# First stage of a hybrid decoder step on one core: order of the first loads, of the turning of x, and of the sum of squares

## The chip, the cores and the metric

The kernel runs on one core of one Trainium2 chip. The metric is the device time in microseconds of one execution; the time before is the median of 3 runs.

## What is computed

One layer of a decoder trunk runs over 256 prompt tokens and 8 sequences of 4 sampled tokens, 288 columns in all (T = 288). The reference, cut to the part that the first stage of the kernel computes (D_MODEL = 2048, all in float32):

```python
mod = (jax.nn.silu(c) @ p['w_ada'] + p['b_ada']).reshape(bsz, 6, 1, D_MODEL)
shift1, scale1, gate1, shift2, scale2, gate2 = (mod[:, i] for i in range(6))

def _rmsnorm(x, g):
    y = x32 * lax.rsqrt(jnp.mean(x32 * x32, axis=-1, keepdims=True) + RMS_EPS)
    return (y * g.astype(jnp.float32)).astype(x.dtype)

h = _rmsnorm(x, p['norm1_g']) * (1 + scale1) + shift1
z = h @ p['w_in']
```

`w_ada` is 2048 x 12288, `w_in` is 2048 x 10528. The rest of the layer (the two token mixers, the gated merge, the output projection, the second norm with the ConvFFN, the final norm) is the same in both kernels and starts after the first stage.

## The kernel before

Everything is written by hand for five instruction streams (`sp`, `pool`, `act`, `dve`, `pe`), with semaphores between them. The order of the work is the order in which the lines are written.

Weights come in slabs. A slab of `w_ada` is 256 rows by 512 columns (0.5 MB), two k tiles. `ada_load(s)` (L594 ff.) sends for slab s, `ada_slab(s)` on TensorE multiplies it with `scT`, the turned silu(c), into a bank of PSUM. Eight slabs (ADA_K) make 512 columns of mod. `ada_place(s)` gives a slab its place: for the first 16 these are four quarters of `kpage` and four of `ada_d`, used in turn, from slab 16 on `ada_x` (which lies over `xnat`, the natural x) and `ada_d`. `ada_load(s)` for s >= 8 waits until slab s - 8 has been used (`ada_used`); slab 16 waits until all twelve banks of x have been read.

After eight slabs ScalarE copies the bank to `adr` (`ada_rows`), TensorE turns it (`ada_turn`) and VectorE adds the bias into `mod` (`ada_cols`).

x arrives with tokens on the partitions and has to be turned. `turn_bank(bi)` turns four 128-column pieces of x into one PSUM bank (four banks in rotation), and `read_bank(bi)` on VectorE copies the bank to `xT`. There are twelve such banks, three token tiles (the last has 32 tokens) by four quarters of the columns, in the order of the list `banks`; a thirteenth, `par`, holds the small parameters, which the list of loads `PARAM_ROWS` brings to `prow` in 17 small transfers.

ScalarE squares xT by quarters (`squares`), TensorE sums all 16 pieces over the partitions with the matrix "mean" (`means`), ScalarE takes the root (`rms`), VectorE the reciprocal (`rstd`) and x / root (`over_root`, L1406), then `ada_first(0)`, `za_lo(0)`, `ada_first(1)`, `norm_quarter(0)` and `norm_lo(0, 0)`. Here the first product with `w_in` can start.

Of `w_in` the first 3360 columns (stage "za") are computed in 36 units (`za_unit`), each of 36 matmuls of 288 columns, with two slabs of `w_in` of 0.375 MB. Between the units TensorE does two more slabs of `w_ada` (`ada_after`). TensorE does slabs 0 to 19 of `w_ada` ahead of the first unit (AHEAD = 20). The sequence of SyncE's queue sets when each slab is sent for:

```python
            for s in range(4):
                ada_load(s)
            ...
            for s in range(4, 8):
                ada_load(s)
            sp.wait_ge(zeroed, 2)
            for name, (t, r, n) in PARAM_ROWS.items():
            ...
            for s in range(8, ADA_EARLY):
                ada_load(s)
```

Of the kernel before, what the change touches and what calls it, by code (L numbers as in the profile page):

```python
# [24 lines left out]
ALU = mybir.AluOpType  # L25
# [6 lines left out]
P = 128  # L32
# [3 lines left out]
T = TP + NB * TS  # L36
# [96 lines left out]
def build(nc, d):  # L133
    ctx = ExitStack()
    with ctx:  # L135
# [384 lines left out]
        for name, ks, groups in (("za", 2, UNITS), ("rest", RS, KA - 1), ("merge", 8, 4), ("out", 8, 4),  # L520
# [10 lines left out]
        ADA_ROWS1 = 1  # L531


        banks = [("x", (m, q)) for m in range(3) for q in range(4)] + [("par", None), ("sh", None)] \
            + [("cv", q) for q in range(2)]
        BANKS_X = 12
        CV_PARTS = [(0, 5), (5, CV_T)]
        ADA_ORDER = [0, 4, 1, 5, 2, 6, 3, 7]
        M_ROWS = [P, P, NB * TS]
# [41 lines left out]
        def _(sp):  # L581
# [15 lines left out]
            def ada_load(s):  # L597

                place, landed_, _ = ada_place(s)
                col = ADA_ORDER[s // ADA_K] * CH  # L600
                if s >= 8 and not ADA_EARLY <= s < ADA_EARLY + 4:
                    sp.wait_ge(ada_used, s - 7)
                sp.dma_start(place.rearrange("p (t n) -> p t n", t=2),
                             wsrc(d["w_ada"], s % ADA_K * 2 * P, col, CH)).then_inc(landed_, 16)
# [4 lines left out]
                wait = (ada_used, 9 + n) if n < 4 else (slab_lo, n - 3)  # L609
                slab(n, 0, 0, wsrc(d["w_in"], (4 * q + 2 * k) * P, u * QT * P, QT * P), wait)  # L610

            for s in range(4):
                ada_load(s)
            for mt in range(2):
                sp.dma_start(xnat[:, mt, :], d["x_prompt"][0, mt * P:(mt + 1) * P, :]).then_inc(x_in, 16)
            sp.dma_start(xnat[0:NB * TS, 2, :], d["x_sample"].rearrange("b t f -> (b t) f")).then_inc(x_in, 16)
            sp.dma_start(cst[:, P:], d["consts"][:, P:]).then_inc(params_in, 16)
            for s in range(4, 8):
                ada_load(s)
            sp.wait_ge(zeroed, 2)  # L620
            for name, (t, r, n) in PARAM_ROWS.items():
                dst = prow[r:r + n, t, :]
                if name == "mu_shift":
                    sp.dma_start(prow[r:r + n - 1, t, :], d[name][0:(n - 1) * P].rearrange("(r c) -> r c", c=P)).then_inc(params_in, 16)
                    w = ZA - (n - 1) * P
                    sp.dma_start(prow[r + n - 1:r + n, t, 0:w], d[name][(n - 1) * P:ZA].rearrange("(r c) -> r c", r=1)).then_inc(params_in, 16)
                elif name == "rwkv_rk":
                    sp.dma_start(dst, d[name].rearrange("(r a) c -> r (a c)", a=2)).then_inc(params_in, 16)
                elif name.startswith("conv_w"):
                    sp.dma_start(dst, d["conv_w"][int(name[-1]), :].rearrange("(r c) -> r c", c=P)).then_inc(params_in, 16)  # L630
                else:
                    sp.dma_start(dst, d[name].rearrange("(r c) -> r c", c=P)).then_inc(params_in, 16)
            for s in range(8, ADA_EARLY):
                ada_load(s)
            sh0 = (SH_T - 1) * P
            sp.dma_start(shnat[0:NB, 0:sh0], d["state_shift"][:, 0:sh0]).then_inc(states_in, 16)
            sp.dma_start(shnat[NB:2 * NB, 0:ZA - sh0], d["state_shift"][:, sh0:ZA]).then_inc(states_in, 16)
            sp.dma_start(cvnat[:, :], d["state_conv"].rearrange("b r (x k) -> (b r x) k", x=4)).then_inc(x_in, 16)
# [219 lines left out]
        def pbank(b):  # L858
            return ps[:, b, :]
# [85 lines left out]
        def _(act):  # L945
# [2 lines left out]
                return act.activation(o, i, ACT.Copy, **k)  # L948


            act.wait_ge(bank_turned, 1)
            act.activation(scT[:, :, 0:NC], pbank(0)[:, 0:KD * NC].rearrange("p (k c) -> p k c", c=NC), ACT.Silu).then_inc(silu_done, 1)

# [34 lines left out]
            def ada_rows(n):  # L988

                act.wait_ge(ada_used, n * ADA_K + ADA_K)  # L990
                if n:
                    act.wait_ge(ada_turned, n)
                copy(adr[:, :], pbank(6 if n else 5)).then_inc(ada_copied, 1)
# [5 lines left out]
            def za_hi(n):  # L999
                hi("za", G(0, None, n // 2), n % 2, QT * P)  # L1000

            ada_rows(0)
            for q in range(4):
                act.wait_ge(bank_read, BANKS_X - 3 + q)
                squares(0, q)
            act.wait_ge(means_done, 1)
            act.activation(rms[:, :], pbank(0)[:, 0:T], ACT.Sqrt, bias=c("eps_rms")).then_inc(rms_done, 1)
            ada_rows(1)
# [341 lines left out]
        def _(dve):  # L1350
# [131 lines left out]
                    ins = TTn(zs, zs, samp(ps[:, b3 + k, TP:T]), ALU.add)  # L1482
                ins.then_inc(za_in_sbuf, 1)

            for bi in range(BANKS_X + 1):
                read_bank(bi)
            inverse_roots(0)
            for q in range(4):
                own.inc(over_root(0, q))
# [454 lines left out]
        def _(pe):  # L1944
# [69 lines left out]
                if q == 3:  # L2014
                    i.then_inc(means_done, 1)

            for k in range(ADA_K):
                ada_slab(k)
                if k >= 4:
                    for bi in range(2 * k - 8, 2 * k - 6):  # L2020
                        turn_bank(bi)
            for k in range(ADA_K):
                ada_slab(ADA_K + k)
                if k < 2:
                    turn_bank(8 + 2 * k)
                    turn_bank(9 + 2 * k)
                if k == 3:
                    turn_bank(BANKS_X)
                if k >= 4:
                    means(0, k - 4)  # L2030
            ada_turn(1, 7)
            for s in range(ADA_EARLY, AHEAD):
                ada_slab(s)
                if s == ADA_EARLY:
                    pe.wait_ge(ada_in_mod, 1)
                    ada_turn(2, 7)
            pe.wait_ge(rms_done, 1)
            pe.wait_ge(bank_read, BANKS_X + 1)

# [599 lines left out]
```

## Time and profile before

| | |
|---|---|
| median of 3 runs | 2440.32 us (2436.37 to 2441.68) |
| the profiled execution, its own time | 2434.05 us |
| its span, first to last instruction | 2432.2 us |
| mean granted clock of TensorE | 0.973 |
| TensorE matmul busy | 2309.8 us, 95% of the span |
| weight loads busy | 2037.3 us, 84% |
| VectorE busy | 1150.6 us, 47% |
| ScalarE busy | 955.8 us, 39% |

Busy times are shares of the whole span. The queue row "q1" carries what SyncE issues (450.39 MB, 59.1% of the sixteen DMA engines' time), "q10" what ScalarE issues (8.38 MB, 1.0%). The granted clock is given as a share of 2.4 GHz: 1.00 is 2.4, 0.50 is 1.2.

### The profile page before, as it was taken

What the parts mean: (1) busy time and instruction counts of PE and PEld (TensorE: products, weight loads), DVE (VectorE), ACT (ScalarE), POOL (GpSimd) and SP (SyncE); (2) the same over time, 40 slices, a digit from 0 to 9 for tenths busy, and PEclk for the clock granted to TensorE, in tenths of its full rate; (3) what the DMA queues carried; (4) which work ended last, traced back from release to release, by engine and by line L of the source; (5) the groups of instructions that cost most, each with busy time, mean ns of one, the idle gap of its engine ahead of it and who ended that gap; (6) DMA issues with size and microseconds to landing.
All of it is one profiled execution on the core that took longest, in us unless ns stands there. A gap on an engine that the chain in (4) does not pass through costs nothing. (4 is left out here: it accounts for less than half of the span.)

```text
span 2432.2 us, 49500 instructions
## 1 busy us (share of the span) xinstructions
PE 2309.8 (95%) x19762; PEld 2037.3 (84%) x19762; DVE 1150.6 (47%) x1908; ACT 955.8 (39%) x1413; POOL 107.6 (4%) x224
## 2 busy tenths in 40 slices
PE   6999899999999999978998999799999999999998
PEld 3789787878878887645666999799999999999998
DVE  3456635344353543434444555645455555544433
ACT  1433333334343343325433333355454554433333
POOL 0000011010000000100000000000000010000000
PEclk8999999999999999959998999899999999999999
DMA  9885556655666656666997555355555555555544
GB/s 316 276 304 150 150 182 183 187 170 180 185 190 187 183 172 189 209 206 228 342 327 249 157 156 165 100 165 165 165 166 166 166 164 164 164 166 164 164 145 119
DMA packets 326693, 461.17 MB, mean 190 GB/s; under 512 B 37338, under 2 KB 220396, under 8 KB 326076
## 3 DMA queue, kind: packets, MB, share of 16 engines
q1 hardware_dynamic: 318893, 450.39, 59.1%
q10 hardware_dynamic: 7634, 8.38, 1.0%
q8 instruction: 128, 2.10, 0.4%
q14 instruction: 38, 0.30, 0.0%
HBM read 442.83 MB, written 15.86 MB: 189 GB/s over the span
## 5 line engine op out<-in xcount | busy, mean ns | idle before, releaser
L948 ACT ACTIVATE whi<-raw 128x1024 fp32r<-128x1024 f32 (+1 forms) x512 | 526.3, 1028 | 912.3 <-PE ps L1948 882.5
L1948 PE MATMUL ps<-hhi,whi 128*128 128x288 f32 x2736 | 832.6, 304 | 12.1 <-DVE hlo L1447 6.4
L1948 PE MATMUL ps<-hhi,wlo 128*128 128x288 f32 x2736 | 808.4, 295 | 0.0
L1948 PE MATMUL ps<-hlo,whi 128*128 128x288 f32 x2736 | 807.6, 295 | 0.0
L1396 DVE TENSOR_TENSOR wlo<-raw,whi 128x1024 fp32r<-128x1024 f32 (+1 forms) x400 | 470.4, 1177 | 624.6 <-ACT whi L948 624.6
L1948 PEld LDWEIGHTS ps<-hhi,whi 128*128 128x128 f32 x2736 | 515.3, 188 | 76.2 <-issue 55.8
L1948 PEld LDWEIGHTS ps<-hlo,whi 128*128 128x128 f32 x2736 | 515.8, 189 | 1.2
L1948 PEld LDWEIGHTS ps<-hhi,wlo 128*128 128x128 f32 x2736 | 515.2, 188 | 0.0
L1948 PE MATMUL ps<-fhi,whi 128*128 128x288 f32 x704 | 208.0, 295 | 2.8 <-DVE wlo L1396 2.8
L1948 PE MATMUL ps<-fhi,wlo 128*128 128x288 f32 x704 | 207.7, 295 | 0.0
L1948 PE MATMUL ps<-flo,whi 128*128 128x288 f32 x704 | 207.3, 294 | 0.0
L1577 DVE TENSOR_TENSOR wlo<-raw,whi 128x1024 fp32r<-128x1024 f32 x112 | 136.7, 1221 | 109.7 <-ACT whi L948 109.6
L1948 PEld LDWEIGHTS ps<-fhi,whi 128*128 128x128 f32 x704 | 132.1, 188 | 3.6 <-DVE wlo L1396 3.5
L1948 PEld LDWEIGHTS ps<-flo,whi 128*128 128x128 f32 x704 | 132.1, 188 | 0.2
L1948 PEld LDWEIGHTS ps<-fhi,wlo 128*128 128x128 f32 x704 | 132.1, 188 | 0.0
L1948 PE MATMUL ps<-raw,scT 128*32 128x512 f32 x512 | 80.7, 634 | 11.9 <-DMA raw<-in_w_ada 11.9
L1948 PE MATMUL ps<-mhi,whi 128*128 128x288 f32 x256 | 76.4, 298 | 1.6 <-DVE wlo L1396 1.6
L948 ACT ACTIVATE kT<-ps 128x1024 f32<-128x1024 f32 x64 | 64.6, 1019 | 32.6 <-PE ps L2494 32.3
L1948 PE MATMUL ps<-mlo,whi 128*128 128x288 f32 x256 | 75.7, 296 | 0.0
L1948 PE MATMUL ps<-mhi,wlo 128*128 128x288 f32 x256 | 75.2, 294 | 0.0
L948 ACT ACTIVATE Xs<-ps 128x256 f32<-128x256 f32 (+1 forms) x48 | 18.4, 383 | 144.2 <-PE ps L1948 144.0
L1661 DVE TENSOR_TENSOR Tn<-Tn,ps 128x128 f32<-128x128 f32 x40 | 11.5, 288 | 122.5 <-PE ps L1948 122.5
(389 smaller groups left out, 2801.0 us busy)
## 6 DMA issues: line engine op xcount, KB each, us to landing
raw<-in_w_up SPq DMA_DIRECT2D x352, 256.0 KB, 2.9
raw<-in_w_ada SPq DMA_DIRECT2D x128, 512.0 KB, 4.9
raw<-in_w_in SPq DMA_DIRECT2D x112, 512.0 KB, 4.6
raw<-in_w_down SPq DMA_DIRECT2D x88, 512.0 KB, 3.9
kpage<-in_cache_v SPq DMA_DIRECT2D x64, 512.0 KB, 5.1
raw<-in_w_in SPq DMA_DIRECT2D x72, 384.0 KB, 5.4
kpage<-in_cache_k SPq DMA_DIRECT2D x40, 512.0 KB, 5.1
ada_d<-in_w_ada SPq DMA_DIRECT2D x32, 512.0 KB, 4.9
```

What stands on the lines that cost most here:

```text
L948: return act.activation(o, i, ACT.Copy, **k)
L1396: TTn(wlo[:, n % 2, :, 0:width], raw[:, n % 4, :, 0:width], whi[:, n % 2, :, 0:width].bitcast(F32), ALU.subtract).then_inc(slab_lo, 1)
L1577: TTn(wlo[:, n % 2, :, :], raw[:, r, :, :], whi[:, n % 2, :, :].bitcast(F32), ALU.subtract).then_inc(slab_lo, 1)
L1661: TTn(even, even, pbank(1)[:, 0:2 * H].rearrange("p (n t) -> p n t", t=1 << lev), ALU.subtract).then_inc(t_done, 1)
L1948: return pe.matmul(out, lhsT, rhs, start=start, stop=stop, **k)
```

## The change

Five things are changed, all ahead of the first unit of "za".

1. SyncE sends for x (three transfers) ahead of slabs 0 to 3.
2. The 17 small parameter transfers are issued by ScalarE, ahead of its first activation, and no longer by SyncE between slabs 7 and 8. The wait on `zeroed` that stood before them stands now, on SyncE, before the states.
3. The banks of x are in the order of quarters (q outside, token tile inside), and TensorE turns all twelve ahead of slab 0; before, two banks stood behind each of slabs 4 to 9.
4. ScalarE squares a quarter as soon as its three banks are read, ahead of `ada_rows(0)`. VectorE adds the four quarters of squares into the first (three additions of 128 x 1152). TensorE then needs 4 matmuls for the mean, behind slab 5, where it had 16 behind slabs 12 to 15.
5. `ada_turn(1)` stands behind slab 11 and `ada_turn(2)` ahead of slab 16; they stood behind slab 15 and behind slab 16.

```diff
-        banks = [("x", (m, q)) for m in range(3) for q in range(4)] + [("par", None), ("sh", None)] \
+        banks = [("x", (m, q)) for q in range(4) for m in range(3)] + [("par", None), ("sh", None)] \
...
+        SQUARES_SUMMED = 2 + 3
...
-            for s in range(4):
-                ada_load(s)
             for mt in range(2):
                 sp.dma_start(xnat[:, mt, :], d["x_prompt"][0, mt * P:(mt + 1) * P, :]).then_inc(x_in, 16)
             sp.dma_start(xnat[0:NB * TS, 2, :], d["x_sample"].rearrange("b t f -> (b t) f")).then_inc(x_in, 16)
+            for s in range(4):
+                ada_load(s)
             sp.dma_start(cst[:, P:], d["consts"][:, P:]).then_inc(params_in, 16)
             for s in range(4, 8):
                 ada_load(s)
-            sp.wait_ge(zeroed, 2)
-            for name, (t, r, n) in PARAM_ROWS.items():
...
             for s in range(8, ADA_EARLY):
                 ada_load(s)
             sh0 = (SH_T - 1) * P
+            sp.wait_ge(zeroed, 2)
...
+            act.wait_ge(zeroed, 1)
+            for name, (t, r, n) in PARAM_ROWS.items():
...
+            for q in range(4):
+                act.wait_ge(bank_read, 3 * q + 3)
+                squares(0, q)
             ada_rows(0)
-            for q in range(4):
-                act.wait_ge(bank_read, BANKS_X - 3 + q)
-                squares(0, q)
...
-            for bi in range(BANKS_X + 1):
+            for bi in range(BANKS_X):
                 read_bank(bi)
+            for q in range(1, 4):
+                dve.wait_ge(squares_done, q + 1)
+                own(TTn(sqs[0][:, 0:4, :], sqs[0][:, 0:4, :], sqs[0][:, 4 * q:4 * q + 4, :], ALU.add))
+            read_bank(BANKS_X)
...
-            for k in range(ADA_K):
-                ada_slab(k)
-                if k >= 4:
-                    for bi in range(2 * k - 8, 2 * k - 6):
-                        turn_bank(bi)
-            for k in range(ADA_K):
-                ada_slab(ADA_K + k)
-                if k < 2:
-                    turn_bank(8 + 2 * k)
-                    turn_bank(9 + 2 * k)
+            for bi in range(BANKS_X):
+                turn_bank(bi)
+            for k in range(ADA_EARLY):
+                ada_slab(k)
                 if k == 3:
                     turn_bank(BANKS_X)
-                if k >= 4:
-                    means(0, k - 4)
-            ada_turn(1, 7)
+                if k == 5:
+                    pe.wait_ge(dve_done, SQUARES_SUMMED)
+                    for t in range(4):
+                        i = mm(pbank(0)[:, 0:T], c("mean"), sqs[0][:, t, :], t == 0, t == 3)
+                    i.then_inc(means_done, 1)
+                if k == ADA_K + 3:
+                    ada_turn(1, 7)
+            pe.wait_ge(ada_in_mod, 1)
+            ada_turn(2, 7)
             for s in range(ADA_EARLY, AHEAD):
                 ada_slab(s)
-                if s == ADA_EARLY:
-                    pe.wait_ge(ada_in_mod, 1)
-                    ada_turn(2, 7)
```

TensorE, from behind the turning of c to the parameters' bank. `kpage` and `ada_d` in the output's place hold slabs of `w_ada` (two matmuls each), `xnat` is x being turned (four transposes to a bank), `prow` the parameters. Before:

```order
2 L1948 MATMUL ps<-kpage,scT 32x512 x8
3 L1948 MATMUL ps<-ada_d,scT 32x512 x2
4 L1978 MATMUL ps<-cst,xnat 128x128 x8
5 L1948 MATMUL ps<-ada_d,scT 32x512 x2
6 L1978 MATMUL ps<-cst,xnat 128x128 x8
7 L1948 MATMUL ps<-ada_d,scT 32x512 x2
8 L1978 MATMUL ps<-cst,xnat 128x128 x8
9 L1948 MATMUL ps<-ada_d,scT 32x512 x2
10 L1978 MATMUL ps<-cst,xnat 128x128 x8
```

The same place with the change, up to the matmuls of the mean (`sq`):

```order
7 L1985 MATMUL ps<-cst,xnat 128x32 x4
8 L1985 MATMUL ps<-cst,xnat 128x128 x8
9 L1985 MATMUL ps<-cst,xnat 128x32 x4
10 L1955 MATMUL ps<-kpage,scT 32x512 x8
11 L1973 MATMUL ps<-cst,prow 128x128 x4
12 L1955 MATMUL ps<-ada_d,scT 32x512 x4
13 L1955 MATMUL ps<-sq_74,cst 128x288 x4
14 L1955 MATMUL ps<-ada_d,scT 32x512 x4
15 L1955 MATMUL ps<-kpage,scT 32x512 x8
```

All 48 transposes of x stand now ahead of the first slab, and the mean stands between slabs 5 and 6 with 4 matmuls.

SyncE's queue from the constants to the first slabs of `w_in` (`raw`), with the change (before, `kpage` x4 stood ahead of `xnat`, and 17 transfers to `prow` between `ada_d` x4 and the second `kpage` x4):

```order
5 L614 DMA xnat<-in_x_prompt 128x2048 x2
6 L615 DMA xnat<-in_x_sample 32x2048
7 L604 DMA kpage<-in_w_ada 128x2x512 x4
8 L618 DMA cst<-in_consts 128x2643
9 L604 DMA ada_d<-in_w_ada 128x2x512 x4
10 L604 DMA kpage<-in_w_ada 128x2x512 x4
11 L604 DMA ada_d<-in_w_ada 128x2x512 x4
12 L625 DMA shnat<-in_state_shift 8x1664
13 L626 DMA shnat<-in_state_shift 8x1696
14 L627 DMA cvnat<-in_state_conv 64x1408
15 L593 DMA raw<-in_w_in 128x2x384 x4
16 L604 DMA ada_x<-in_w_ada 128x2x512 x4
```

What is loaded ahead of the first unit, and from slab 8 on its order, is as before.

ScalarE, from behind the parameters to the root, with the change (`scT` is silu(c), which every slab and, through a wait, every turning of x stands behind):

```order
12 L946 DMA prow<-in_mu_shift 1x32
13 L952 DMA prow<-in_conv_b 44x128
14 L950 DMA prow<-in_conv_w 44x128 x3
15 L955 ACT_TABLE_LOAD
16 L955 ACTIVATE scT<-ps 128x16x9
17 L968 ACTIVATE sq_74<-xT 128x1152 x4
18 L937 ACTIVATE adr<-ps 128x512
19 L1010 ACT_TABLE_LOAD
20 L1010 ACTIVATE rms<-ps,cst 128x288
```

Silu and its table load stood first on this engine; the 17 issues of small transfers are now ahead of them, and the squares ahead of the first copy to `adr`.

## Rows read from the trace of the kernel before

**Rows 1.** Timeline of TensorE, first stage: start us, duration us, what, count, idle before.

```profile
21.66 1.92 PE L1948 MATMUL ps<-ada_d,scT 128*32 128x512 f32 x4 [9.83 <-DMA ada_d<-in_w_ada]
23.51 1.95 PE L1978 MATMUL ps<-cst,xnat 128*128 128x128 f32 x8
26.37 1.09 PE L1978 MATMUL ps<-cst,xnat 128*128 128x128 f32 x8
...
37.16 2.21 PE L1948 MATMUL ps<-sq,cst 128*128 128x288 f32 x8
...
50.36 1.05 PE L1948 MATMUL ps<-ada_x,scT 128*32 128x512 f32 x4 [0.84 <-ACT adr L948]
56.73 1.88 PE L1948 MATMUL ps<-cst,adr 128*128 128x9 f32 x8 [5.32 <-DVE mod L1388]
58.54 3.63 PE L1948 MATMUL ps<-ada_x,scT 128*32 128x512 f32 x12
64.31 0.37 PE L1948 MATMUL ps<-hhi,whi 128*128 128x288 f32 x1 [2.14 <-DVE hlo L1452]
```

**Rows 2.** Timeline of VectorE, first stage.

```profile
27.07 1.29 DVE L1373 COPY xT<-ps 128x512 f32<-128x512 f32 x2 [0.88 <-PE ps L1978]
...
49.30 1.95 DVE L1401 RECIPROCAL rstd<-rms 128x288 f32<-128x288 f32 x1 [12.32 <-ACT rms L1007]
51.29 5.17 DVE L1406 TENSOR_TENSOR sq<-xT,rstd 128x1152 f32<-128x1152 f32 x4
56.48 0.20 DVE L1388 TENSOR_TENSOR mod<-ps,par 128x36 f32<-128x36 f32 x1
56.60 0.95 DVE L1396 TENSOR_TENSOR wlo<-raw,whi 128x768 fp32r<-128x768 f32 x1
58.65 0.20 DVE L1388 TENSOR_TENSOR mod<-ps,par 128x36 f32<-128x36 f32 x1 [1.10 <-PE ps L1948]
```

**Rows 3.** Timeline of ScalarE, first stage.

```profile
37.53 1.28 ACT L1007 ACT_TABLE_LOAD   x1
48.77 0.50 ACT L1007 ACTIVATE rms<-ps,cst 128x288 f32<-128x288 f32 x1 [9.96 <-PE ps L1948]
```

**Rows 4.** Timeline of SyncE's queue: start and duration of issues.

```profile
10.24 6.84 SPq L632 DMA_DIRECT2D prow<-in_b_ada  x1
```

**Rows 5.** Single transfers: issue ns, start us; us to landing (second: least, median, most of x's three).

```profile
L616 SPq DMA_DIRECT2D xnat<-in_x_sample x1: 432/432/432, 5.1 to 5.1; - x1
...
DMA to landing us min/median/max: 8.5/11.1/12.2
...
L603 SPq DMA_DIRECT2D ada_d<-in_w_ada x1: 2694/2694/2694, 7.5 to 7.5; - x1
...
DMA to landing us min/median/max: 18.4/18.4/18.4
...
L603 SPq DMA_DIRECT2D kpage<-in_w_ada x1: 389/389/389, 23.1 to 23.1; - x1
...
DMA to landing us min/median/max: 6.4/6.4/6.4
...
L592 SPq DMA_DIRECT2D raw<-in_w_in x1: 398/398/398, 32.5 to 32.5; - x1
...
DMA to landing us min/median/max: 12.2/12.2/12.2
```

**Rows 6.** The last slab of w_ada ahead of the first unit, the same columns.

```profile
L603 SPq DMA_DIRECT2D ada_x<-in_w_ada x1: 1792/1792/1792, 41.3 to 41.3; - x1
...
DMA to landing us min/median/max: 12.0/12.0/12.0
```

**Rows 7.** Windows: stretch; busy of PE, PEld, DVE, ACT, POOL; PEclk, DMA share, GB/s.

```profile
14.00:16.00 2.00, 0.00 (x0) 0.00 (x0) 0.00 (x0) 0.00 (x0) 0.00 (x0) 0.77 1.14 219
...
54.00:56.00 2.00, 0.00 (x0) 0.00 (x0) 2.00 (x2) 0.00 (x0) 0.00 (x0) 0.50 1.05 386
...
80.00:90.00 10.00, 10.00 (x79) 8.14 (x78) 3.08 (x5) 4.37 (x9) 0.00 (x0) 1.00 0.88 302
```

More of the change, by code:

```diff
@@ L619, in _ @@
                 ada_load(s)
-            sp.wait_ge(zeroed, 2)
-            for name, (t, r, n) in PARAM_ROWS.items():
[L622 to L632, printed above, removed]
             for s in range(8, ADA_EARLY):
@@ L948, in copy @@
                 return act.activation(o, i, ACT.Copy, **k)
+            act.wait_ge(zeroed, 1)
+            for name, (t, r, n) in PARAM_ROWS.items():
+                dst = prow[r:r + n, t, :]
+                if name == "mu_shift":
+                    act.dma_start(prow[r:r + n - 1, t, :], d[name][0:(n - 1) * P].rearrange("(r c) -> r c", c=P)).then_inc(params_in, 16)
+                    w = ZA - (n - 1) * P
+                    act.dma_start(prow[r + n - 1:r + n, t, 0:w], d[name][(n - 1) * P:ZA].rearrange("(r c) -> r c", r=1)).then_inc(params_in, 16)
+                elif name == "rwkv_rk":
+                    act.dma_start(dst, d[name].rearrange("(r a) c -> r (a c)", a=2)).then_inc(params_in, 16)
+                elif name.startswith("conv_w"):
+                    act.dma_start(dst, d["conv_w"][int(name[-1]), :].rearrange("(r c) -> r c", c=P)).then_inc(params_in, 16)
+                else:
+                    act.dma_start(dst, d[name].rearrange("(r c) -> r c", c=P)).then_inc(params_in, 16)
             act.wait_ge(bank_turned, 1)
```

## Prediction, on record before the changed kernel was run

> **What bounds the kernel now.** The page's section 1 comes first: TensorE is busy for 95% of the span, so time can be won only where it stands still. One such place is the first stage, and the timeline of TensorE shows it [rows 1]: the engine waits until 21.66 us for slab 4 of w_ada, and after slab 16 (50.36, 1.05 us) it does nothing until 56.73, waits again from 62.2 (58.54 + 3.63) and starts the first unit of "za" at 64.31. From there the windows show it busy without a gap, 10.00 of 10 us at full clock, with the DMA engines at 0.88 [rows 7]. So the first stage is worth what the start at 64.31 moves, and nothing else in the program hangs on absolute time.
>
> Next I ask what ends last before 64.31. The timelines of VectorE and ScalarE [rows 2, 3] show one chain: the last mean ends at 48.7, root at 48.77 (0.50), reciprocal 49.30 (1.95), x over root 51.29 (5.17), the first bias 56.48; TensorE turns the second group (56.73, 1.88), bias 58.65, and the normed quarter with its splitting into high and low parts takes until 64.31, 5.66 us after 58.65. 15.6 us of chain, all behind the mean. It is VectorE and ScalarE that bound the start now.
>
> Behind them stands the stream of loads. Landing times are issue plus time to landing [rows 5]: x complete at 5.1 + 12.2 = 17.3, slab 7 at 7.5 + 18.4 = 25.9, slab 8 at 23.1 + 6.4 = 29.5, the first slab of w_in at 32.5 + 12.2 = 44.7, and slab 19, the last that TensorE needs ahead of the first unit, at 41.3 + 12.0 = 53.3 [rows 6]. From 44.7 to 53.3 three slabs of w_in and four of w_ada land, 3.3 MB, that is 1.36 us for a slab of w_ada. The window 54 to 56 has the DMA engines at 1.05 and 386 GB/s while TensorE is idle [rows 7]: the stream has run full all the time. This is the floor under whatever the chain may win.
>
> **The change, part by part.**
>
> *x ahead of slabs 0 to 3.* x lands four slabs sooner: 17.3 - 4 x 1.36 = 11.9, and 12.5 with half a microsecond for the parameters' bytes beside it.
>
> *Parameters on ScalarE.* 17 issues. On SyncE the list took from 10.24 to 23.1; 6.84 of it was the first, which stood before a full queue [rows 4, 5], so the other 16 took 6.0, 0.37 each. On ScalarE 17 x 0.37 = 6.3 us from about 1.4, to 7.7; then the table load (1.28) and silu (0.3, my estimate from the 0.50 of the root, a smaller tile): 9.4. TensorE starts nothing before silu, but x lands at 12.5, so 3 us are left. The issues are hidden by x's landing; without that cover each microsecond of list beyond 10.8 is a microsecond of turning.
> In the stream the list cost more than its 0.19 MB: slab 8 landed 3.6 us behind slab 7, where 1.36 is usual, 2.2 too many. Issued early they fall partly into the first microseconds, before anything large is queued. The ends: the whole 2.2 goes, or nothing. I take 1.0. In a sentence by itself: the Trainium skill, "DMA: Bandwidth & Descriptors", section "Issuing engines are not separate DMA queues", says that transfers from several engines share the same 16 DMA engines and spreading saves only the issuing time; by that the stream would win nothing, slab 19 stays at 53.3 and the gain is one microsecond smaller than below.
>
> *Turning x first.* Twelve banks. When TensorE is warm VectorE sets the pace, 1.29 for two banks [rows 2], 0.65 each; cold, the transposes do, 1.95 for two, against 1.09 warm [rows 1]. Between 6 and 12.5 the engine is idle, and an idle engine lost its clock before (0.77 in 14 to 16, 0.50 in 54 to 56) [rows 7]. Ends 7.8 (all warm) and 11.7 (all cold); I take four banks cold, 3.9 + 5.2 = 9.1, since before the clock was back within three rows of taking up work. x is turned at 21.6.
>
> *Does the late start of the slabs starve the stream?* Slab 8 may be sent for when slab 0 is used: 21.6 + 1.05 = 22.7. By then everything up to slab 7 is queued, which keeps the engines busy until about 26.3 (25.9 plus the parameters' bytes). 3.6 us of cover, so nothing lost. TensorE then uses a slab in 1.05 where the stream brings one in 1.36; the mean and the parameters' bank (2.21 and 0.7) fit.
>
> *Squares, sums, mean.* The last square follows the last bank (1.1 us), the last addition (1.29, as one of the four 128 x 1152 operations at 51.29) ends at 24.0. Slabs 0 to 5 with the parameters' bank are done at 21.6 + 6 x 1.05 + 0.7 = 28.6; 4 matmuls for the mean, 2.21 (eight rows of the trace are four matmuls) [rows 1]: 30.8. Twelve matmuls less are 6.6 us of TensorE, but in a stretch where it will wait anyway: counted at nothing. ScalarE must first copy group 0 (slab 7 at 32.9, 0.60), then load a table 1.28, root 0.50: 35.3. Reciprocal 1.95, over root 5.17: 42.5; first bias 42.7. Before, this was 56.7: the chain has won 14.0.
>
> *What is late next.* VectorE's next step needs the high part of the first w_in slab: 44.7 - 1.0 = 43.7 landed, 44.5 copied (0.8), low part 45.4 (0.95), then 5.66 as before: 51.1. And slab 19: lands 52.3. If TensorE has lost its clock, the slab takes 1.9 (as at 21.66), else 1.05: done at 54.2 or 53.4. The later of 51.1 and 54.2 is the stream's. **First unit at 54.2 instead of 64.3: 10.1 us less.**
>
> *Does the stage after it keep the gain?* Units need the fifth slab of w_in at about 54.2 + 4.7 + 2.1 + 4.7 + 2.1 + 0.8 = 68.6 (36 matmuls at 0.13, from the 79 in 10 us [rows 7], for a unit; two slabs of w_ada between, the shift bank), less 1.8 for splitting: 66.8. It lands behind slabs 20 to 27 and one of its own kind: 52.3 + 8 x 1.36 + 1.0 = 64.2. Cover 2.6 us.
>
> Sum against the profiled execution: 2434.05 - 10.1 = 2423.9. That execution lies 6.3 below the median; the difference is applied to the median: 2440.3 - 10.1 = 2430.2.
>
> **The rivals.** About 0.2% (4.9 us) is what a measurement of this kernel can tell from no change.
>
> *A, the issues of both engines hold each other up.* One issue can stand for 6.84 us [rows 4]. If the generator of descriptors serves one engine at a time, ScalarE's 6.3 and SyncE's 9 us of issuing up to 10.2 lie behind each other: list done at 14, silu 15.6, x turned 24.7, slab 8 sent for at 25.8, just before the queue is empty, and landing at 30 (4 us later) instead of 27.7. Slab 19 at 54.6, first unit 56.5: 2432.5. For: full queue in the trace. Against: ScalarE's ring is its own. The Trainium skill, "Perfetto Trace Analysis", section "Per-engine timelines", tells of such a lock on the generator for one engine at a time; no run here shows it yet.
>
> *B, the stream gets faster.* The parameters' 2.2 us go whole and TensorE keeps its clock: slab 19 at 51.1, done at 52.2, with the chain at 49.9: 12.1 less, 2428.2.
>
> *C, part is given back in "za".* If w_in's fifth slab comes after 66.8 because the stream has no lead at the start any more, TensorE waits; bounded by 3.5 us, as each pair of slabs of both weights takes 4.8 us of stream and 6.8 of TensorE, so the lead grows again. 2433.7. For: the start moves and the stream does not.
>
> *D, slower.* ScalarE's list is held behind the full queue as SyncE's was, and silu with it, on which every slab and all turning hangs. If the list ends at L, x is turned at L + 10.7, slab 8 lands at L + 16, the first unit starts at L + 42.5. Level with before at L = 21.8; slower by 0.2% from L = 26.7. The 8 MB ahead of it land by 26.3, so L = 29 is its natural end: start 71.5, 2447.5. For: that same row [rows 4]. Against: the first parameter met a queue with some 5 MB in it, ScalarE's first is issued before SyncE has 1 MB in.
>
> *E, no difference.* As D with L between 17 and 26: 2440.
>
> **How the numbers follow.** Forecast 0.54, A 0.13, B 0.11, C 0.12, D 0.03, E 0.07. A, B, C and the forecast are all faster by over 4.9, C and A with two noisy medians less surely: faster 0.85, same 0.11, slower 0.04. The range takes in B with the 2.7 us by which the runs before differ (2425.5) and C with the same (2436.5).
>
> **What would show it.** Right: x's last landing near 12.5; ScalarE's list over by 8 to 9; transposes in one block from 12.5 to 22; no DMA window under 0.9 between 4 and 54; root near 35; TensorE waiting last for ada_x, and first w_in product at 54 +/- 1.5; from there the same trace, shifted. Wrong: gaps between ScalarE's issues (A, D); the last wait before the first product naming VectorE (chain, not stream, is the bound); waits for whi or wlo in the second to fourth unit (C).

## The result, and the profile after

| | before | after |
|---|---|---|
| median | 2438.76 us, 4 runs (2436.37 to 2441.68) | 2413.65 us, 4 runs (2410.91 to 2415.36) |
| profiled execution, its own time | 2434.05 us | 2410.91 us |
| its span | 2432.2 us | 2409.1 us |
| granted clock, mean | 0.973 | 0.978 |

The ratio is 0.9895, with a 95% interval of 0.9878 to 0.9913. The kernel is 25.1 us faster by the medians, 23.1 by the spans of the two profiled executions. The forecast was 10.1, and the measured time lies below the range.

Section 1 of the page after: each engine's busy time, share of the span, records.

```profile
PE 2297.0 (95%) x19738; PEld 2029.4 (84%) x19738; DVE 1154.4 (48%) x1911; ACT 956.5 (40%) x1413; POOL 105.2 (4%) x224
```

TensorE has 24 records fewer than before (x19762) in both of its rows (a record is one instruction as the profile lists it): the 12 matmuls of the mean that are gone, each in two passes with a weight load for each, 48 instructions in all. Its waits and register instructions are as many in both kernels. That count matters further down.

**The first stage.** Timeline of TensorE, after (start us, duration us, what, count, idle before):

```profile
12.52 8.21 PE L1985 MATMUL ps<-cst,xnat 128*128 128x128 f32 x48 [6.08 <-DMA xnat<-in_x_sample]
20.66 1.92 PE L1955 MATMUL ps<-kpage,scT 128*32 128x512 f32 x16
22.51 0.66 PE L1973 MATMUL ps<-cst,prow 128*128 128x128 f32 x4
23.09 2.07 PE L1955 MATMUL ps<-ada_d,scT 128*32 128x512 f32 x8
25.55 2.21 PE L1955 MATMUL ps<-sq,cst 128*128 128x288 f32 x8 [0.39 <-DVE sq L1492]
...
48.16 4.58 PE L1955 MATMUL ps<-ada_x,scT 128*32 128x512 f32 x12 [3.04 <-DMA ada_x<-in_w_ada]
53.18 1.05 PE L1955 MATMUL ps<-ada_x,scT 128*32 128x512 f32 x4 [0.45 <-DMA ada_x<-in_w_ada]
54.17 0.40 PE L1955 MATMUL ps<-hhi,whi 128*128 128x288 f32 x1
```

These rows answer to [rows 1]. The first product of "za" starts at 54.17, where it was 64.31. The last two waits ahead of it are for slabs of w_ada: the stream of loads is what ends last.

Timelines of VectorE and of ScalarE, after:

```profile
21.37 4.13 DVE L1492 TENSOR_TENSOR sq<-sq 128x1152 f32<-128x1152 f32 x3
...
31.29 1.95 DVE L1404 RECIPROCAL rstd<-rms 128x288 f32<-128x288 f32 x1 [5.07 <-ACT rms L1010]
33.28 5.17 DVE L1409 TENSOR_TENSOR sq<-xT,rstd 128x1152 f32<-128x1152 f32 x4
38.48 0.20 DVE L1391 TENSOR_TENSOR mod<-ps,par 128x36 f32<-128x36 f32 x1
...
49.39 1.36 DVE L1455 TENSOR_TENSOR hlo<-sq,hhi 128x1152 fp32r<-128x1152 f32 x1 [0.36 <-ACT hhi L937]
```

```profile
7.67 1.21 ACTq L950 DMA_DIRECT2D prow<-in_conv_w  x3
8.91 1.28 ACT L955 ACT_TABLE_LOAD   x1 [8.91 <-issue]
10.20 0.30 ACT L955 ACTIVATE scT<-ps 128x144 f32<-128x144 f32 x1
...
28.85 0.60 ACT L937 ACTIVATE adr<-ps 128x512 f32<-128x512 f32 x1 [6.20 <-PE ps L1955]
29.46 1.28 ACT L1010 ACT_TABLE_LOAD   x1
30.76 0.50 ACT L1010 ACTIVATE rms<-ps,cst 128x288 f32<-128x288 f32 x1
```

The root [rows 3] has moved from 48.77 to 30.76, the first bias [rows 2] from 56.48 to 38.48. The chain's last piece, hlo, ends at 49.39 + 1.36 = 50.75, ahead of the last slab.

The last slab of w_ada ahead of the first unit, after (answers to [rows 6]):

```profile
L604 SPq DMA_DIRECT2D ada_x<-in_w_ada x1: 3052/3052/3052, 39.1 to 39.1; - x1
...
DMA to landing us min/median/max: 14.0/14.0/14.0
```

39.1 + 14.0 = 53.1, where before it landed at 53.3. The stream itself has won 0.2 us; what has won is everything that stood behind it.

Windows of after (stretch; busy of PE, PEld, DVE, ACT, POOL; PEclk, DMA share, GB/s; answers to [rows 7]):

```profile
6.00:12.00 6.00, 0.44 (x5) 0.35 (x4) 0.00 (x0) 1.59 (x2) 0.00 (x0) 1.00 1.01 321
...
20.00:36.00 16.00, 14.97 (x84) 5.08 (x82) 10.79 (x12) 4.71 (x5) 0.00 (x0) 1.00 1.07 387
36.00:48.00 12.00, 4.82 (x16) 2.12 (x16) 6.02 (x18) 2.28 (x3) 0.00 (x0) 0.62 1.05 277
```

The DMA share is full throughout. The 1.00 of the window 6 to 12 is no reading of the clock: the trace's first clock record starts at 18.4 us (1.00, the upper level, 2.4 GHz), and ahead of a first record the column prints 1.00. How fast TensorE ran ahead of it stands in the transposes themselves. Here are the first eight and, behind 18.4 us, seven of the same form (ns of one, least, median, most; first and last start in us):

```profile
L1985 PE MATMUL ps<-cst,xnat x8: 421/421/447, 12.5 to 14.0; 128*128 128x128 f32 x8
...
L1985 PE MATMUL ps<-cst,xnat x7: 272/273/273, 19.4 to 20.1; 128*128 128x128 f32 x7
```

So the engine began x at the lower level: the first two banks took 1.94 us, as the slow row of [rows 1] (1.95). The records change from 421 to 273 ns at 18.3 to 18.5 us. The clock fell again to 0.50 at 38.9 us, in the later waits (0.62 in 36 to 48), and was back at 52.6.

**Where the other 13 us are.** The first stage gives 10.14 us, as forecast. The forecast's other half, "from there the same trace, shifted", does not hold. I measured the same landmarks in both traces (the start of the first unit, the first record that turns `nsh`, the first copy of each `v_thw` in the loop of the RWKV mixer, then `kT`, the first product of the output projection, `ynat`):

| stretch | before | after | difference |
|---|---|---|---|
| start to the first unit of "za" | 64.31 | 54.17 | -10.14 |
| "za", to nsh and to the first v_thw | 208.1 + 11.6 | 208.3 + 11.6 | +0.2 |
| seven rounds of the RWKV mixer | 720.3 | 711.0 | -9.3 |
| last v_thw to kT | 102.3 | 99.2 | -3.1 |
| kT to the output projection, and from there to ynat | 232.3 + 1082.2 | 232.0 + 1082.0 | -0.5 |

9.3 us come out of seven rounds whose code the diff does not touch. The chain that ended last is no help here (it names three pieces near the end of the span). The table of waits over those rounds is: before, 284.06 to 1004.41, then after, 274.11 to 985.12 (engine and tile, what it waited for: total us, times, longest).

```profile
ACT whi L948 <- DMA raw<-in_w_in: 27.1, 7, 4.5
...
PEld ps L1948 <- DMA raw<-in_w_ada: 17.1, 7, 3.3
...
PE ps L1948 <- DMA raw<-in_w_ada: 10.8, 7, 2.4
```

```profile
ACT whi L937 <- DMA raw<-in_w_in: 23.1, 7, 3.7
...
PEld ps L1955 <- DMA raw<-in_w_ada: 10.6, 7, 1.9
...
PE ps L1955 <- DMA raw<-in_w_ada: 4.3, 6, 1.0
```

Once in each round TensorE waits for a slab of w_ada, and this wait is 6.5 us shorter over the seven. It is the slab that SyncE sends for 9.5 us after the round's first v_thw. The third round shows it at its largest: its wait, 2.4 us, is the longest of before's seven (10.8 / 7 = 1.5 at the mean). Windows of the DMA queues, before at 499 to 501 us and after at 486 to 488 us, the same place of the round (queue: packets, MB, share of 16 engines; then the issues, KB, us to landing):

```profile
q1 hardware_dynamic: 419, 0.25, 56.0%
q8 instruction: 1, 0.02, 3.5%
...
raw<-in_w_ada SPq DMA_DIRECT2D x1, 512.0 KB, 6.7
```

```profile
q1 hardware_dynamic: 445, 0.26, 59.6%
...
raw<-in_w_ada SPq DMA_DIRECT2D x1, 512.0 KB, 4.8
```

Before, one packet of the queue "instruction" (16 KB, 3.5% of 16 engines over 2 us, so 1.1 us of one engine) runs as the slab is sent for. The slab takes 6.7 us, and its issue 1.41 instead of 0.38. After, there is no such packet here; it comes 7.6 us later in the round. The timeline of SyncE and of TensorE before, and then of TensorE after, show what hangs on it:

```profile
499.66 1.41 SPq L678 DMA_DIRECT2D raw<-in_w_ada  x1
```

```profile
506.41 1.80 PE L1948 MATMUL ps<-raw,scT 128*32 128x512 f32 x4 [2.37 <-DMA raw<-in_w_ada]
```

```profile
491.62 1.05 PE L1955 MATMUL ps<-raw,scT 128*32 128x512 f32 x4 [0.45 <-DMA raw<-in_w_ada]
```

TensorE waits 2.37 instead of 0.45 and then works at the lower clock for 3.4 us (1.80 instead of 1.05 for the slab; the window behind it, in before, is below, columns as in [rows 7]). Of before's seven rounds only this one has such a fall of the clock behind the wait for the slab.

```profile
508.00:510.00 2.00, 2.00 (x10) 1.86 (x9) 0.00 (x0) 0.00 (x0) 0.00 (x0) 0.50 0.95 257
```

### The profile page after: what moved, and what is told of

Its sections match the earlier page's. It is cut to its first block and busy times, and to the rows that moved or that the text cites. A ratio compares the mean times of both kernels' runs of the same rounds, so it can differ in the third digit from the quotient of the medians.

```text
span 2409.1 us, 49458 instructions
## 1 busy us (share of the span) xinstructions
PE 2297.0 (95%) x19738; PEld 2029.4 (84%) x19738; DVE 1154.4 (48%) x1911; ACT 956.5 (40%) x1413; POOL 105.2 (4%) x224
## 5 line engine op out<-in xcount | busy, mean ns | idle before, releaser
L1955 PE MATMUL ps<-hhi,whi 128*128 128x288 f32 x2736 | 831.8, 304 | 10.1 <-DVE hlo L1450 6.4
L937 ACT ACTIVATE Xs<-ps 128x256 f32<-128x256 f32 (+1 forms) x48 | 18.4, 383 | 143.3 <-PE ps L1955 143.1
## 6 DMA issues: line engine op xcount, KB each, us to landing
raw<-in_w_up SPq DMA_DIRECT2D x352, 256.0 KB, 2.9
```

What stands on the lines that cost most here:

```text
L1955: return pe.matmul(out, lhsT, rhs, start=start, stop=stop, **k)
```

## The experiments

Eleven runs, each timed beside the kernel before on the same chip: the first four together (before 2432.9 us), then four on another chip (before 2432.66), then three on the first chip again (before 2432.76). Four theories of the rounds stand against each other. Q: what SyncE's queue holds early on sets how its later transfers land. L: it is luck, and differs from one execution to the next. S: the earlier start itself does it. P: TensorE's place in its program does, since its instructions are fetched in blocks.

One correction goes ahead: where an expectation below places an instruction fetch within a round, I had counted the DMA records from their own zero, which lies 10.9 us before the span's start. On the span's clock "+20.5" is +9.6, "+28" is +17, and so on; the table below has the span's clock.

**Is it luck, or which part of the change does it?** Four kernels.

The kernel before, unedited.

> The kernel before, unchanged, for a second trace. Known so far: the first unit of za starts 10.1 us sooner with the change (64.31 to 54.17), as forecast, but the median fell by 25 us; of the 23.1 us between the two profiled spans 9.3 lie in the seven rounds of the RWKV loop (102.9 us a round before, 101.6 after) and 3.4 between that loop and the MoBA stage. Theory Q (queue): what SyncE's queue carried before, 17 small transfers more, sets how its transfers in the later stages land; it is the same in every execution. Then this trace shows rounds of 102.9 again (720 us for seven) and a span near 2432. Theory L (luck): the rounds differ from execution to execution; then this trace shows anything from 711 to 720.

Measured: 2435.23 us (2430.37 to 2437.53), ratio 1.0006 [0.9997, 1.0016]; first unit 63.95, seven rounds 719.7 us. So 720 is a property of the kernel, not of one execution.

The kernel after, with the 17 parameter transfers back on SyncE:

```diff
-            act.wait_ge(zeroed, 1)
-            for name, (t, r, n) in PARAM_ROWS.items():
-                ...
             for s in range(4, 8):
                 ada_load(s)
+            sp.wait_ge(zeroed, 2)
+            for name, (t, r, n) in PARAM_ROWS.items():
+                ...
             for s in range(8, ADA_EARLY):
```

> The changed kernel with the 17 small transfers back on SyncE, where they stood, between slabs 7 and 8. The first stage loses what the list costs in the stream: first unit at 55 to 56.5 instead of 54.2. Theory Q: the later stages are slow again, seven rounds take 720, total 2425 to 2431. Theory S (start: the later gain follows from x first, the turning and the sums, through the earlier start): rounds stay at 711, total 2415 to 2417.

Measured: 2414.13 us (2409.84 to 2417.02), 0.9924 [0.9908, 0.9941]; first unit 54.65, a little ahead of the 55 to 56.5 that I expected, rounds 711.0. SyncE has its old queue again, and the rounds stay short.

The kernel before, with the parameters on ScalarE (the same edit the other way round):

```diff
-            sp.wait_ge(zeroed, 2)
-            for name, (t, r, n) in PARAM_ROWS.items():
-                ...
+            act.wait_ge(zeroed, 1)
+            for name, (t, r, n) in PARAM_ROWS.items():
+                ...
```

> The kernel before with only the 17 small transfers moved to ScalarE. TensorE waits for slab 4 at 21.66 and works back to back from there, so the first unit stays at 62 to 64.5. Theory Q: seven rounds take 711, total 2423 to 2428. Theory S: rounds stay at 720, total 2436 to 2440.

Measured: 2435.84 us, 1.0009 [0.9998, 1.0021]; first unit 66.31, rounds 720.8. SyncE's queue does not decide the rounds. And the move alone wins nothing in the first stage. It loses 2.0 us there, outside the 62 to 64.5 that I expected: slab 4, for which TensorE waits first, lands 1.5 us later (23.1 for 21.6), and the root ends at 51.3 instead of 49.3.

The kernel before, with x ahead of slabs 0 to 3:

```diff
-            for s in range(4):
-                ada_load(s)
             for mt in range(2):
                 sp.dma_start(xnat[:, mt, :], ...)
             sp.dma_start(xnat[0:NB * TS, 2, :], ...)
+            for s in range(4):
+                ada_load(s)
```

> The kernel before with only x sent for ahead of slabs 0 to 3. TensorE's order is the old one: it turns x behind slab 4, which lands at 21.6 as before, so the first unit stays at 64.3. Theory Q: rounds at 720, total 2436 to 2441. Theory S: no earlier start, so no later gain either: the same. A total under 2432 would speak against both.

Measured: 2432.96 us, 0.9996 [0.9987, 1.0006]; first unit 64.46, rounds 718.5. x early is worth nothing while its banks are still turned behind slabs 4 to 9.

What is left of the change is TensorE's order and the 48 instructions fewer, and with them the place of all its later instructions in its program. Most of the bytes on the DMA queues named "instruction" are 16 KB packets on q8, 128 of them (2.10 MB) in both kernels. In the seven rounds they keep step with TensorE's program: 56 packets (57 in one run), one for every 256 of TensorE's records (255.6 in before, 255.8 in after, 255.4 to 256.0 in the other runs). I read each as one fetch of TensorE's instructions. The Trainium skill, "Runtime: NRT & Kernel Launch", section "Instruction fetch mechanics", says that an engine's instructions are refilled in 16 KiB blocks of 256 instructions, and that the cost of crossing a block's end is mostly hidden. The size and the 256 agree with these packets; the cost is what the next runs test.

**Is it TensorE's place in its program?** Four kernels.

The kernel after, unedited.

> The changed kernel, unchanged, for a second trace on this chip. Seven rounds of the RWKV loop took 720.3, 719.7, 720.8 and 718.5 us in the four traces with the old first stage on TensorE, 711.0 and 711.0 in the two with the new one. If that is the kernel's and not chance, it is 710 to 712 here; first unit 54.2 +/- 0.5; total 15 to 22 us under before.

Measured: 2411.82 us (2408.24 to 2419.89), 0.9923 [0.9902, 0.9945]; first unit 51.48, rounds 711.7. The rounds are the kernel's own. The first unit is 2.2 us ahead of the expected band: in this execution slab 19 landed at 50.3 instead of 53.1.

The kernel after with the 48 instructions back, as 12 matmuls of 8 columns that nobody reads:

```diff
             pe.wait_ge(ada_in_mod, 1)
+            pe.wait_ge(rms_done, 1)
+            for t in range(12):
+                mm(pbank(0)[:, 0:8], c("mean"), ident[:, 0:8])
             ada_turn(2, 7)
```

> The changed kernel with 12 tiny matmuls (8 columns, result unused) in TensorE's idle time ahead of ada_turn(2). Theory P (program position): the change took 12 matmuls out of TensorE's straight-line program, 48 machine instructions (a float32 matmul is two loads and two products in the trace), so that the blocks in which TensorE's program is fetched begin at other places of the later work, and the slabs at the head of each RWKV round land sooner. The 12 tiny ones put all later work back to the old place: seven rounds 718 to 721, total 9 to 14 us over the changed kernel, first unit still at 54 to 55. Theory S (the earlier start or the new first stage itself): nothing changes, rounds 711, total within 2 us of the changed kernel.

Measured: 2422.63 us (median of twelve: eleven from 2416.91 to 2427.78, and one of 2976.18), 0.9961 [0.9948, 0.9974]; first unit 55.49, rounds 717.2. 12 tiny matmuls in a stretch where TensorE waits cost 10.8 us against e5. By the two profiles (11.4 us) it is 4.0 to the first unit, 5.5 in the rounds and 4.0 in the stretch up to kT, less 0.3 in "za" and 1.7 behind kT. Of these only the rounds are clear of what two executions of one kernel differ by anyway (2.7 us at the first unit, after and e5; 2.0 in the stretch up to kT, before and e1). The rounds came just under the 718 to 721 of theory P.

The kernel before with 208 instructions more. 208 is 256 less 48, so, if the fetching goes in blocks of 256, from there on every instruction stands against the blocks as in the kernel after:

```diff
                 if s == ADA_EARLY:
+                    pe.wait_ge(rms_done, 1)
+                    for t in range(52):
+                        mm(pbank(0)[:, 0:8], c("mean"), ident[:, 0:8])
                     pe.wait_ge(ada_in_mod, 1)
                     ada_turn(2, 7)
```

> The kernel before with 52 tiny matmuls (208 machine instructions) ahead of ada_turn(2), where TensorE waits. If fetching goes in blocks of 256 instructions, as the 128 transfers of 16 KB on the instruction queue (64 bytes each) would have it, 208 more is the same place as 48 fewer. They may push the first unit from 64.3 to 66 to 72. Theory P: seven rounds fall from 720 to 711. Theory S: they stay at 718 to 721.

Measured: 2442.77 us, 1.004 [1.0024, 1.0057]; first unit 80.88, 16.6 later and far outside the 66 to 72 that I expected, and rounds of 710.6, nearly 10 us shorter than before's, in a kernel that has nothing else of the change. A start that is 16.6 us later also removes the thought that the rounds are short because they start earlier.

The kernel after with its sums back on TensorE: 16 matmuls for the mean, no additions on VectorE, everything else as in after.

```diff
-                    pe.wait_ge(dve_done, SQUARES_SUMMED)
-                    for t in range(4):
-                        i = mm(pbank(0)[:, 0:T], c("mean"), sqs[0][:, t, :], t == 0, t == 3)
-                    i.then_inc(means_done, 1)
+                    for q in range(4):
+                        means(0, q)
...
-            for q in range(1, 4):
-                dve.wait_ge(squares_done, q + 1)
-                own(TTn(sqs[0][:, 0:4, :], sqs[0][:, 0:4, :], sqs[0][:, 4 * q:4 * q + 4, :], ALU.add))
```

> The changed kernel with the 16 matmuls of the mean again (all behind slab 5), without VectorE's three additions. By my account of the first stage the stream of loads bounds the start: the chain ends 4 to 7 us later (root 35 to 37, normed quarter 51 to 53), the first unit stays at 54.2 to 55. TensorE's later program stands at the old place. Theory P: rounds 718 to 721, total 9 to 14 over the changed kernel. Theory S: 711, total within 2.

Measured: 2422.76 us, 0.9962 [0.9946, 0.9978]; first unit 53.96, rounds 720.3. The first stage is as expected: root at 36.7, chain over at 51.5, and the first unit behind slab 19 (landed 52.1) as in after. The additions win nothing there that these profiles can tell (53.96 with 16 matmuls, 54.17 and 51.48 with 4). The kernel loses 10.9 us without them all the same, and 8.6 of it lies in the rounds.

**Other places.** The kernel after with 20, 32 and 52 of the tiny matmuls at the place of e6, and the same diff but for the number. M in the expectations is a rival that had still to be told apart: that any added instruction makes the rounds long.

> The kernel after with 20 matmuls of 8 columns (80 machine instructions) ahead of the second group's bias turning, written to a bank that nothing reads. They cost the first unit 1 to 3 us. P (where TensorE's program stands against the blocks of 256 instructions in which it is fetched decides how long the seven rounds of RWKV take): the fetches, at about +4 and +28 us of a round in the kernel after and at +2 and +20.5 with 48 more, move on to about +16 and late in the round before; the seven rounds together take a value of their own between 710 and 721, and they are as long as the fetch at that place makes them, not simply 717. M (any instructions added to the kernel after make the rounds longer, by whatever way): 717 or more. Time 2415 to 2426.

Measured: 2425.46 us, 0.9965 [0.9951, 0.9979]; first unit 56.80, rounds 714.1.

> As the run with 80 more, with 32 matmuls (128 machine instructions, half a block). The first unit is 3 to 5 us later than in the kernel after. P: fetches at about +9 and +33 of a round, so the w_ada slab issued at +9.5 meets one as it lands or goes free of both: a value of its own between 708 and 722. M: 717 or more. Time 2414 to 2430.

Measured: 2425.91 us, 0.997 [0.9961, 0.9979]; first unit 63.45, rounds 710.5.

> As the run with 80 more, with 52 matmuls (208 machine instructions, which is 48 less than one block: the position of a program with 12 matmuls fewer still). The first unit is 4 to 8 us later. P: fetches at about +10 and +35 of a round: rounds of 709 to 713, as in the kernel after or better. M: 717 or more, the most of the three. Time 2413 to 2432.

Measured: 2432.93 us, 1.0004 [0.9994, 1.0014]; first unit 70.11, rounds 712.4. M wanted 717 or more in all three and has none. P's numbers for the rounds hold; the places of the fetches that it gave do not, even on the span's clock (for +80, +5 against +6.5 to +6.8; for +128, -2 against +3.0 to +3.5). Nor did my price for the tiny matmuls: I gave 3 to 5 us for 32 and 4 to 8 for 52, and the first unit came 9.3 and 15.9 later. The timeline of TensorE in e10 has the reason:

```profile
42.26 13.82 PE L1955 MATMUL ps<-cst 128*128 128x8 f32 x64
```

They run behind the wait at 42 us, with the clock down, at 0.22 us a record, and cover the end of the wait instead of hiding in it. So none of these versions is faster than the kernel after, which has a good place for nothing. In these runs a place bought with idle instructions cost more than it brought.

**All kernels side by side.** "Place" is the number of TensorE's instructions ahead of the rounds, against after, less whole blocks of 256. "Fetch" is when the packet nearest to the slab's issue at +9.5 starts, in us from the round's start, in rounds two to seven. "Wait" is PE's wait for raw<-in_w_ada, and PEld's, over the seven rounds. The first round is left out of the third and fourth columns, since its slab is sent for later (10.1 to 10.9 us); it carries 1.8 of the 9.3 us (103.9 before, 102.1 after).

| kernel | place | fetch | slab's landing, us | wait, PE and PEld | seven rounds |
|---|---|---|---|---|---|
| before | +48 | +9.1 to +9.9 | 5.5 to 6.7 | 10.8, 17.1 | 720.3 |
| e1 before again | +48 | +9.1 to +10.1 | 5.4 to 6.7 | 10.6, 17.0 | 719.7 |
| e3 parameters alone | +48 | +9.0 to +9.8 | 5.4 to 7.1 | 11.8, 18.2 | 720.8 |
| e4 x alone | +48 | +8.9 to +9.8 | 5.3 to 6.3 | 9.8, 16.2 | 718.5 |
| e8 sums by TensorE | +48 | +9.0 to +9.9 | 5.2 to 6.9 | 11.3, 17.7 | 720.3 |
| e6 after, 48 more | +48 | +9.1 to +10.0 | 5.4 to 6.2 | 9.9, 16.2 | 717.2 |
| e9 after, 80 more | +80 | +6.5 to +6.8 | 4.6 to 4.9, sent for 0.4 to 0.8 later | 7.1, 13.5 | 714.1 |
| e11 after, 208 more | +208 | +2.8 to +3.4 in three rounds, +18.9 to +22.3 in three | 4.7 to 5.6 | 4.8, 11.4 | 712.4 |
| after | 0 | +14.4 to +17.1 | 4.6 to 5.4 | 4.3, 10.6 | 711.0 |
| e5 after again | 0 | +14.6 to +17.3 | 4.6 to 5.3 | 3.3, 10.7 | 711.7 |
| e2 parameters on SyncE | 0 | +14.2 to +17.2 | 4.5 to 5.5 | 3.7, 10.2 | 711.0 |
| e7 before, 208 more | 0 | +14.7 to +17.4 | 4.7 to 5.5 | 3.6, 9.9 | 710.6 |
| e10 after, 128 more | +128 | +3.0 to +3.5 | 4.7 to 4.9 | 3.1, 9.7 | 710.5 |

Three pairs of the rows behind the fifth column, from the waits over the seven rounds of e6, e7 and e10:

```profile
PEld ps L1955 <- DMA raw<-in_w_ada: 16.2, 7, 2.8
...
PE ps L1955 <- DMA raw<-in_w_ada: 9.9, 7, 1.9
```

```profile
PEld ps L1948 <- DMA raw<-in_w_ada: 9.9, 7, 2.1
...
PE ps L1948 <- DMA raw<-in_w_ada: 3.6, 6, 1.2
```

```profile
PEld ps L1955 <- DMA raw<-in_w_ada: 9.7, 8, 1.5
...
PE ps L1955 <- DMA raw<-in_w_ada: 3.1, 7, 0.6
```

And the DMA window of e6's third round, 490 to 492 us, where the packet is back, and with it the late slab:

```profile
q8 instruction: 1, 0.02, 3.7%
...
raw<-in_w_ada SPq DMA_DIRECT2D x1, 512.0 KB, 5.7
```

What follows. The six kernels at +48 have rounds of 717 to 721 us together, all others 710.5 to 714.1, whatever else stands in them and whenever they start. PE's wait for the slab is 9.8 to 11.8 us in the six, 3.1 to 4.8 in the six at 0, +128 and +208. In the 36 rounds of the six in which a fetch starts within a microsecond of the slab's issue, the slab takes 5.2 to 7.1 us (median 5.7), and in 23 of them the issue itself 0.95 to 1.8 us. Which of the 36 these are goes by the order: in all 23 the packet had started ahead of the issue, by 0.02 to 0.60 us, and in the other 13, with issues of 0.38, it started 0.07 to 0.56 us behind it. The slab took 5.9 us at the median in the 23 and 5.6 in the 13. In the 36 rounds of the six kernels at 0, +128 and +208 the slab takes 4.5 to 5.6 (median 4.9), and the issue never over 0.4. e9 is between them: its fetch meets the slab before (4.3 to 4.6 us where the others have 3.6 to 4.1), and the one at +9.5 is sent for late. That the place in the program sets the length of the rounds is shown, in both directions. That it does so by the fetch's packet meeting that one slab is read from rows in which the two go together; no run moved the slab and left the fetch.

## Why the prediction was wrong, and where it was right

**The step that failed** is in the first paragraph: "nothing else in the program hangs on absolute time", with its echo, "from there the same trace, shifted". What stands behind the first unit did change, by 13 us in the profiled pair. I looked for an effect of the shifted start, and there was none to find (e7 starts 16.6 us later and has short rounds). What I had not asked is what else the change shifts: TensorE's instructions against the blocks in which they are fetched. "Twelve matmuls less are 6.6 us of TensorE [...] counted at nothing" was right for their work (e8: 53.96 with all 16), and wrong for their absence: e6 and e8 lose 10.8 and 10.9 us against e5. On their chip the whole change is worth 20.8 us. What is shown to be that place is the rounds' share: 9.3 of the 23.1 us in the first pair of profiles, and 5.5 and 8.6 of what e6 and e8 lose. The rest of their loss lies in stretches that differ between two executions of one kernel too. Nothing I read would have told the sign; but rows of the queue "instruction" with their share of 0.4% stood in the profile, and the prediction has no term or rival for them. Its range is therefore too narrow: 2425.5 was my most favourable sum plus noise, with no room for an effect of the code's layout in either direction.

**The first stage**, step by step:

| step | forecast | measured |
|---|---|---|
| x landed | 12.5 | 2.8 + 9.6 = 12.4 |
| ScalarE's list over, silu over | 7.7, 9.4 | 8.9, 10.5 |
| twelve banks turned | 9.1 us, at 21.6 | 8.2 us, at 20.7 |
| six slabs and the parameters' bank | 7.0 us | 20.66 to 25.16, 4.5 us |
| last addition of squares | 24.0 | 25.5 |
| root done | 35.3 | 31.3 |
| first bias | 42.7 | 38.5 |
| chain over (hlo) | 51.1 | 50.75 |
| slab 19 landed | 52.3 | 53.1 |
| first unit | 54.2 | 54.17 |

The sum is right to 0.03 us, and part of that is luck: e5, the same kernel, starts its first unit at 51.48, 2.7 us earlier, since its slab 19 landed at 50.3. The single terms were off by more, in both directions.

- *Clock and banks.* I took four banks of twelve cold. Seven were: the transposes took 0.42 us each until 18.3 us and 0.27 from 18.5 on. The term came out short all the same, at 8.2 for 9.1, because I had priced the four banks of 32 tokens like the others: two of them take 0.68 us in before where two full ones take 1.09. Two errors of opposite sign met here, which is luck too.
- *Slabs that are already there.* I gave each 1.05 us from [rows 1]; four of them took 1.92 together. Rows of a slab that is waited for do not price one that is not. With that the mean no longer stood behind slab 5 but waited for VectorE's additions. Of these I had counted one behind the last bank; all three stand there, 4.13 us, because VectorE was reading banks until then.
- *Root.* 4 us early, mostly because slab 7, behind which ScalarE copies the first group, was done at 28.8 and not at 32.9. It won nothing more at the first unit, which waits for slab 19.
- *The parameters' bytes.* I took 1.0 us of stream; slab 19 came 0.2 sooner. The sentence from the Trainium skill ("DMA: Bandwidth & Descriptors", "Issuing engines are not separate DMA queues") was nearer: it had slab 19 at 53.3. e2, with the parameters back on SyncE, has it at 53.2. But e5 has 50.3 without any change, so a term of 1 us cannot be told from these profiles either way. The times (2414.13 for e2, 2411.82 for e5, beside befores of 2432.9 and 2432.66) do not part the two either.
- *Stream and cover.* The DMA share stays at 1.01 to 1.07 through the late start of the slabs, and "za" takes 208.3 us where it took 208.1: nothing is given back. Rivals A, C, D and E did not happen. Of A only a hint is seen: the 17 issues took 0.44 us each, where I had 0.37.

Rival B had the stream 2 us faster and gave 2428.2; e5's profile is of that kind, but that is 2 us of the missing 13 at most.

**Still open:** the 3.1 us between the last v_thw and kT (102.3 before, 99.2 after; 99.2 to 104.3 in the other runs, without an order that I can name, and 100.3 in both e1 and e5, so that 2 us of it pass between executions of before alone), and why the stream brings slab 19 at 53.1 in one execution of the same kernel and at 50.3 in another. Also open is a stretch of the record: from 1603 to 2077 us of after (1623 to 2097 of before) no packet of q8 is listed. It lies behind the rounds, and nothing here rests on it.

## What to carry to other kernels

When an engine's program is streamed in and its loads run close to its work, adding or removing a few instructions early on moves every later fetch. In this kernel the rounds differed by up to 10 us of 2430 with it, as much as the first stage won. Before crediting an edit with what it won, run it once more with its instructions put back where they do nothing, and look whether the stretches that it does not touch stay as long as they were. A matter of layout is not kept by the next edit, so the part of a gain that comes from it should be named as such.

## What the runs showed of the hardware

- One 16 KB packet of the queue "instruction" holds one DMA engine for 1.1 us (3.5% of 16 engines in 2 us). A 512 KB slab sent for within 0.6 us of it lands 0.8 us later at the median, at most 2.2 (7.1 against 4.9). Where the packet started first, SyncE's issue took 0.95 to 1.8 us instead of 0.38, and the packet itself 1.13 at the median instead of 0.93. The Trainium skill, "Runtime: NRT & Kernel Launch", section "Instruction fetch mechanics", calls the cost of a new block mostly hidden. Hidden it is where nobody waits for the slab: after's own packet, 493.5 to 495.5 us, falls on a slab that takes 6.6 us, and no wait follows from it.
- The seven rounds are 9.3 us longer in before, more than the 6.5 us that TensorE's wait for this slab grows. TensorE stands still for 16.7 us of them in before and 9.4 in after, and is busy 703.6 and 701.6 us with the same 7100 records. The idle part goes with the place (15.2 to 16.9 us at +48, 8.1 to 9.9 at 0, +128 and +208). The busy part does so less surely: e5 has 703.2 at place 0, e6 702.0 at +48. A fall of the clock behind the wait adds to it in single rounds (1.80 for a slab instead of 1.05, in before's third).
- Matmuls of 8 columns with 128 x 128 weights took 0.22 us a record at the lower clock (e10), four records to a matmul in float32 with its weight loads counted: filler is not free on TensorE.
